# Sample-state steps moved from the levels of the triangular inverses to the steps of the chunk chain (RWKV-7 stage of a hybrid decoder trunk)

## Chip, cores, metric

One NeuronCore of one Trainium2 chip. The metric is the device time of one execution in microseconds (us). The time before is the median of three runs.

## What is computed

A two-layer trunk runs over 256 prompt tokens and 32 sample tokens (8 sequences of 4 tokens each, the "last tokens"). Layer 0 is a chunked gMLP unit and a SwiGLU. Layer 1 is RWKV-7 time mixing with 16 heads of 64, and then a top-2-of-8 expert SwiGLU. The change lies in the RWKV-7 recurrence:

```
def step(s, inp):
    r_t, w_t, k_t, v_t, kk_t, a_t = inp
    s_kk = jnp.einsum("bhij,bhj->bhi", s, kk_t)
    s = (s * w_t[:, :, None, :]
         - s_kk[..., None] * (kk_t * a_t)[:, :, None, :]
         + v_t[..., None] * k_t[:, :, None, :])
    y = jnp.einsum("bhij,bhj->bhi", s, r_t)
    return s, y
```

The prompt starts from a zero state. Each of the 8 samples starts from its own state (16 heads of 64x64). The outputs and the last states of both are outputs of the kernel.

## The kernel before

Every engine has its own instruction queue, written out in the order of the program. The recurrence isn't run token by token. The prompt is cut into four chunks of 64 tokens. Inside a chunk the recurrence becomes a triangular system, so the stage has three parts:

- **Scores and inverses.** For each half `i` (two chunks, all 16 heads), the step `score` makes the products of keys and queries, `xt0` and `x0` start an inverse, and five levels `t1/i/m`, `xl/i/m` (m = 1 to 5) build it up. A `t1` is a product that ScalarE copies out of PSUM in two halves (L1028). An `xl` is the product that follows, which VectorE copies by a mask into the inverse (L1545). On TensorE (PE) a `t1` is L2198 and an `xl` is L2213.
- **The chunk chain.** For chunk `c` = 0 to 3: `w1` (L2151, L2228, L2236), `u` (L2260 with L2247 and L2252), `s` (L2279) and `y` (L2288, L2291, L2294). Each one's result is copied out of PSUM (ScalarE L1033, L1038, L1043; VectorE L1551, L1556, L1569) before a later one reads it. From `c` = 1 on, `w1` has a second part that takes the same state to `y`, and `u` has products behind the ones that are copied.
- **The samples.** The steps whose names begin with `q_` do the same for the 32 sample tokens. `q_xt0`, `q_x0`, `q_t1` and `q_x2` are their small inverse. `q_s0/p` (p = 0 to 7, a pair of heads) turns the loaded states with four 128x128 transposes into bank 6 (L2343), from which ScalarE copies them (L1058). `q_qs/p` is the state times the sample's rows, 16 small matmuls a step with 2x4 = 8 moving columns each (L2351); after four of them ScalarE copies the sum (`Qs`, L1064), and GpSimd scales the state (L755). Then come `q_w1/g`, `q_u/g`, `q_y/g` (g = 0, 1 is a group of 8 heads; PE L2363 and L2367, L2375, L2384), and `q_st/p`, which makes the last state (PE L2401, L2409; ScalarE L1076) that four DMAs on SyncE's queue store (L592). GpSimd makes the key blocks of `q_st` (L739).

After the chain come the group norm (`gm`, `gv`: L2419, L2428) with `q_st/4` to `q_st/7` between its steps, then `gate`, `state` and the output projection `wo`.

What sets the order is one list, `steps` (L407 to L433). The main steps are appended one after the other by `then`, and after each one the next entry of the list `fill` is appended, which holds the sample steps. All engines walk the same list, each issuing its share of every step. The waits are worked out from the list, so a step that is moved keeps its own waits:

```
        def then(step):
            steps.append(step)
            steps.extend(fill.pop(0))
```

Bank 6 is one buffer, so a step `q_s0` waits until the copy of the one before has read it:

```
                    elif p == 4:
                        q_wait(pe, "q_qc", 0)
                    else:
                        q_wait(pe, "q_s0c", p - 1)
```

Of the kernel before, what the change touches and what calls it, by code (L numbers as in the profile page):

```python
# [54 lines left out]
def trunk_kernel(nc, a, out):  # L55

    with ExitStack() as ctx:
# [339 lines left out]
        def norm_dve(k, gain, dst):  # L397
            nc.vector.wait_ge(S["rinv_ready"], k)
            for c in range(DC):
# [7 lines left out]
        steps = [("score", 0, g_) for g_ in range(4)] + [("xt0", 0), ("q_score", 0), ("x0", 0), ("q_score", 1)]  # L407
        fill = [[("score", 1, 0)], [("score", 1, 1)], [("score", 1, 2)], [("score", 1, 3)], [("xt0", 1), ("q_xt0", 0)],
                [("q_x0", 0)], [("q_s0", 0)], [("q_t1", 0)], [("q_s0", 1)], [("q_x2", 0)],
                [("q_s0", 2)], [("q_x0", 1)], [("q_s0", 3)], [("q_t1", 1)], [("q_qs", 0), ("q_qs", 1)], [("q_x2", 1)],  # L410
                [("q_qs", 2), ("q_qs", 3)], [("q_w1", 0)], [], [("q_u", 0)], [("q_y", 0)],
                [("q_s0", 4)], [("q_s0", 5)], [("q_s0", 6)], [("q_s0", 7)],
                [("q_qs", 4), ("q_qs", 5)], [("q_qs", 6), ("q_qs", 7)], [("q_w1", 1)], [("q_st", 0)],
                [("q_u", 1)], [("q_st", 1)], [("q_y", 1)], [("q_st", 2)], [], [("q_st", 3)], [], []]

        def then(step):
            steps.append(step)
# [2257 lines left out]
```

## Time and profile before

| | |
|---|---|
| runs, us | 1540.66, 1546.23, 1542.77 (median 1542.77) |
| profiled execution: its own time, us | 1537.36 |
| its span, us | 1535.6 |
| TensorE busy | 1493.6 us (97%) |
| VectorE, ScalarE, GpSimd busy | 71%, 56%, 8% |
| mean granted TensorE clock | 0.992 |

The trace splits each of this stage's f32 matmuls in two records, so a step with 32 matmuls has 64 records. Ends of matmuls overlap the starts of the next by about 0.07 us in the timeline; the chain of waits cuts this overlap off.

### The profile page before, as it was taken

How to read it: one execution, taken by the hardware profiler on the slowest of the kernel's cores; microseconds unless marked ns; L12 is line 12 of the kernel's file. 1: busy time of each engine (PE TensorE's matmuls, PEld its weight loads, DVE VectorE, ACT ScalarE, POOL GpSimd, SP SyncE). 2: the span in 40 equal slices, each digit the busy share in tenths (PEclk: the TensorE clock that was granted, in tenths of full speed). 3: DMA queues.
4: the chain of work that ended last, by engine and by line, in shares of the span. 5: the costliest groups of instructions: out<-in, count | busy, mean ns of one | idle time of the engine just before them, and what ended most of it. 6: DMA issues, size and time to landing. Idle time of an engine off the chain costs nothing.

```text
span 1535.6 us, 26614 instructions
## 1 busy us (share of the span) xinstructions
PE 1493.6 (97%) x11533; PEld 1219.1 (79%) x11533; DVE 1090.4 (71%) x1053; ACT 857.2 (56%) x838; POOL 130.5 (8%) x170
## 2 busy tenths in 40 slices
PE   7999999999999979999999999999999999999997
PEld 7999999999889768976667777777777777777774
DVE  5687455554468664222498888888889889888897
ACT  5444444433264323232367777777777777777775
POOL 0065100000100030142000000000000000000010
PEclk9999999999999999999999999999999999999999
DMA  8643575535255020055599999999999999999992
GB/s 261 186 138 83 164 228 165 165 114 160 74 164 166 1 58 4 21 127 182 193 313 390 377 381 371 367 388 373 376 369 373 382 381 376 367 380 367 385 388 89
DMA packets 250269, 378.05 MB, mean 246 GB/s; under 512 B 28169, under 2 KB 142073, under 8 KB 249858
## 3 DMA queue, kind: packets, MB, share of 16 engines
q1 hardware_dynamic: 247874, 370.04, 69.5%
q0 software_dynamic: 2064, 6.18, 1.2%
q8 instruction: 93, 1.52, 0.4%
q14 instruction: 30, 0.25, 0.1%
q10 hardware_dynamic: 208, 0.07, 0.0%
HBM read 368.47 MB, written 7.78 MB: 245 GB/s over the span
## 4 chain that ended last, share of the span: by engine, by line
PE 94%; DVE 3%; issue 1%; ACT 1%; DMA 0%; ACTq 0%; DVEq 0%
PE bank L2552 46%; PE bank L1916 27%; PE bank L2039 3%; PE bank L2213 1%; PE bank L2198 1%; DVE wL L1609 1%; PE bank L2460 1%; PE bank L2485 1%; PE bank L2561 1%; PE bank L1969 1%; PE bank L2409 1%; PE bank L2533 1%; PE bank L2401 0%; PE bank L2351 0%; PE bank L2260 0%
## 5 line engine op out<-in xcount | busy, mean ns | idle before, releaser
L1609 DVE TENSOR_TENSOR wL<-ering,wH 128x2048 fp32r<-128x2048 f32 x264 | 603.6, 2289 | 87.7 <-ACT wH L1102 86.3
L1102 ACT ACTIVATE wH<-ering 128x2048 fp32r<-128x2048 f32 x264 | 506.0, 1917 | 152.4 <-PE bank L2552 151.5
L2552 PE MATMUL bank<-wH,xgH 128*96 128x512 f32 (+1 forms) x768 | 290.2, 378 | 3.1 <-DVE wL L1609 2.8
L2552 PE MATMUL bank<-wH,xgL 128*96 128x512 f32 (+1 forms) x768 | 287.3, 374 | 0.0
L2552 PE MATMUL bank<-wL,xgH 128*96 128x512 f32 (+1 forms) x768 | 286.9, 374 | 0.0
L2552 PEld LDWEIGHTS bank<-wH,xgH 128*96 128x96 f32 x768 | 124.4, 162 | 46.5 <-issue 3.1
L2552 PEld LDWEIGHTS bank<-wH,xgL 128*96 128x96 f32 x768 | 124.2, 162 | 43.9
L2552 PEld LDWEIGHTS bank<-wL,xgH 128*96 128x96 f32 x768 | 124.5, 162 | 41.4
L2552 PE MATMUL bank<-wH,hH 128*96 128x512 f32 x352 | 139.5, 396 | 0.5 <-DVE wL L1609 0.5
L2552 PE MATMUL bank<-wH,hL 128*96 128x512 f32 x352 | 138.3, 393 | 0.0
L2552 PE MATMUL bank<-wL,hH 128*96 128x512 f32 x352 | 137.9, 392 | 0.0
L906 ACT ACTIVATE fwH<-fring 128x2048 fp32r<-128x2048 f32 (+1 forms) x38 | 64.2, 1690 | 116.8 <-PE bank L1916 116.8
L1352 DVE TENSOR_TENSOR fwL<-fring,fwH 128x2048 fp32r<-128x2048 f32 (+1 forms) x38 | 76.4, 2011 | 42.7 <-ACT fwH L906 42.7
L1916 PE MATMUL bank<-fxH,fwH 128*128 128x288 f32 x352 | 104.4, 297 | 0.0
L1916 PE MATMUL bank<-fxH,fwL 128*128 128x288 f32 x352 | 103.8, 295 | 0.0
L1916 PE MATMUL bank<-fxL,fwH 128*128 128x288 f32 x352 | 103.5, 294 | 0.0
L1916 PE MATMUL bank<-inH,inW 128*128 128x288 f32 x256 | 77.3, 302 | 0.5 <-DVE inL L1298 0.5
L2552 PEld LDWEIGHTS bank<-wH,hL 128*96 128x96 f32 x352 | 56.7, 161 | 24.7
L2552 PEld LDWEIGHTS bank<-wH,hH 128*96 128x96 f32 x352 | 56.8, 161 | 24.6 <-DVE wL L1609 1.4
L1916 PE MATMUL bank<-inH,lowW 128*128 128x288 f32 x256 | 76.1, 297 | 0.0
L1916 PE MATMUL bank<-inL,inW 128*128 128x288 f32 x256 | 75.9, 296 | 0.0
L2552 PEld LDWEIGHTS bank<-wL,hH 128*96 128x96 f32 x352 | 56.9, 162 | 22.8
(431 smaller groups left out, 2557.3 us busy)
## 6 DMA issues: line engine op xcount, KB each, us to landing
ering<-m_w_gate SPq DMA_DIRECT2D x88, 1024.0 KB, 7.0
ering<-m_w_up SPq DMA_DIRECT2D x88, 1024.0 KB, 7.4
ering<-m_w_down SPq DMA_DIRECT2D x88, 1024.0 KB, 7.4
arena<-a_w_in SPq DMA_DIRECT2D x16, 1024.0 KB, 5.7
arena<-b_w_rkv SPq DMA_DIRECT2D x12, 1024.0 KB, 5.2
fring<-f_w_gate SPq DMA_DIRECT2D x11, 1024.0 KB, 5.4
fring<-f_w_up SPq DMA_DIRECT2D x11, 1024.0 KB, 5.3
fring<-f_w_down SPq DMA_DIRECT2D x16, 704.0 KB, 4.7
```

What stands on the lines that cost most here:

```text
L906: nc.scalar.activation(fw[n % FRING][0][:, 0:w], fring[:, (F_GU + n) % RING, 0:w], ACT.Copy) \
L1102: s_.activation(wH[:, hslot(g), :], ering[:, eslot(g), :], ACT.Copy).then_inc(S["e_hi"], 1)
L1352: v.tensor_tensor(fw[n % FRING][1][:, 0:w], fring[:, (F_GU + n) % RING, 0:w], fw[n % FRING][0][:, 0:w].bitcast(F32), ALU.subtract).then_in ...
L1609: v.tensor_tensor(wL[:, hslot(g), :], ering[:, eslot(g), :], wH[:, hslot(g), :].bitcast(F32), ALU.subtract).then_inc(S["e_lo"], 1)
L1916: mm = t.matmul(bank[:, 0:T], w2[l], x2[r][:, k, :], start=(start and m == 0), stop=(stop and m == 2))
L1969: mm = t.matmul(banks[c % 4][:, t0:t0 + n], vtok[0:n, i, P * c:P * c + P], w, start=False, stop=True, skip_group_check=True)
L2039: mm = t.matmul(bank, w(k), x[:, k, :], start=(k == 0), stop=(k == ks - 1))
L2198: mm = t.matmul(banks[3 * f][far, 64 * j:64 * j + 64], MS[ch, BL, i, 8 * f + j, :], X[ch, 8 * f + j, :], start=(j == 0), stop=True, skip_g ...
L2213: mm = t.matmul(banks[1 + 3 * f + x][ch if x else far, 64 * j:64 * j + 64], pair[x], pair[1 - x], start=(j == 0), stop=True, skip_group_ch ...
L2409: mm = t.matmul(bank[:, P * q:P * q + P], S0[p][:, 2 * q:2 * q + 2, :].rearrange("p b i -> p (b i)"), ident[:, :], start=False, stop=True, ...
L2460: mm = t.matmul(banks[4 + c][:, 0:T], wo[c // 2][:, k_, P * (c % 2):P * (c % 2) + P], yT[:, k_, :], start=(k_ == 0), stop=(k_ == DC - 1))
L2552: mm = t.matmul(dst, lhs[l], rhs[r], start=(start and m == 0), stop=(stop and m == 2), skip_group_check=True)
```

## The change

Only the list `fill` changes. `q_qs/0` to `q_qs/3`, `q_w1/0`, `q_u/0` and `q_y/0` no longer stand between the levels of the second inverse (`t1/1/m`, `xl/1/m`), but between the steps of the chain. What stood in the chain moves down by up to several steps to make room: `q_st/0` to `q_st/3` move down by two steps of the chain each, `q_st/3` from between `u/3` and `s/3` to behind `y/3`. `q_s0/4` and `q_s0/5` now follow each other directly. From `gm/0` on both lists are the same, and so is everything up to `xl/1/2`.

```diff
@@ -407,11 +407,10 @@
         steps = [("score", 0, g_) for g_ in range(4)] + [("xt0", 0), ("q_score", 0), ("x0", 0), ("q_score", 1)]
         fill = [[("score", 1, 0)], [("score", 1, 1)], [("score", 1, 2)], [("score", 1, 3)], [("xt0", 1), ("q_xt0", 0)],
                 [("q_x0", 0)], [("q_s0", 0)], [("q_t1", 0)], [("q_s0", 1)], [("q_x2", 0)],
-                [("q_s0", 2)], [("q_x0", 1)], [("q_s0", 3)], [("q_t1", 1)], [("q_qs", 0), ("q_qs", 1)], [("q_x2", 1)],
-                [("q_qs", 2), ("q_qs", 3)], [("q_w1", 0)], [], [("q_u", 0)], [("q_y", 0)],
-                [("q_s0", 4)], [("q_s0", 5)], [("q_s0", 6)], [("q_s0", 7)],
-                [("q_qs", 4), ("q_qs", 5)], [("q_qs", 6), ("q_qs", 7)], [("q_w1", 1)], [("q_st", 0)],
-                [("q_u", 1)], [("q_st", 1)], [("q_y", 1)], [("q_st", 2)], [], [("q_st", 3)], [], []]
+                [("q_s0", 2)], [("q_x0", 1)], [("q_s0", 3)], [("q_t1", 1)], [], [("q_x2", 1)], [], [], [], [], [],
+                [("q_qs", 0), ("q_qs", 1)], [("q_qs", 2), ("q_qs", 3)], [("q_w1", 0)], [("q_s0", 4), ("q_s0", 5)],
+                [("q_u", 0), ("q_s0", 6)], [("q_s0", 7)], [("q_y", 0), ("q_qs", 4), ("q_qs", 5)], [("q_qs", 6), ("q_qs", 7)],
+                [("q_w1", 1)], [("q_st", 0)], [("q_u", 1)], [("q_st", 1)], [("q_y", 1)], [("q_st", 2)], [], [("q_st", 3)]]
```

The list is one line shorter, so all later lines have a number that is one lower in the changed kernel (L2213 is L2212 there).

**First place:** TensorE at the second inverse, from `xl/1/2` to `w1/0`. Before (L2213 is `xl`, L2351 `q_qs`, L2198 `t1`, L2330 `q_x2`, L2363 and L2367 `q_w1`, L2375 `q_u`, L2384 `q_y`, L2151 `w1`):

```order
L2213 MATMUL bank<-arena 64x64 x64
L2351 MATMUL bank<-arena 64x2x4 x32
L2198 MATMUL bank<-arena 64x64 x32
L2330 MATMUL bank<-arena 32x32 x8
L2213 MATMUL bank<-arena 64x64 x64
L2351 MATMUL bank<-arena 64x2x4 x32
L2198 MATMUL bank<-arena 64x64 x32
L2363 MATMUL bank<-arena 32x64 x8
L2367 MATMUL bank<-ident,arena 32x128 x4
L2213 MATMUL bank<-arena 64x64 x64
L2198 MATMUL bank<-arena 64x64 x32
L2375 MATMUL bank<-arena 32x64 x8
```

The same stretch of the changed kernel, up to `u/0`:

```order
L2212 MATMUL bank<-arena 64x64 x64
L2197 MATMUL bank<-arena 64x64 x32
L2329 MATMUL bank<-arena 32x32 x8
L2212 MATMUL bank<-arena 64x64 x64
L2197 MATMUL bank<-arena 64x64 x32
L2212 MATMUL bank<-arena 64x64 x64
L2197 MATMUL bank<-arena 64x64 x32
L2212 MATMUL bank<-arena 64x64 x32
L2150 MATMUL bank<-arena 64x64 x32
L2350 MATMUL bank<-arena 64x2x4 x32
```

Only `q_x2/1` is left between the levels, `w1/0` follows the last level directly, and the first `q_qs` pair comes behind `w1/0`.

**Second place:** TensorE behind `y/0` (its last products are L2294, L2293 in the changed kernel), up to `w1/1`. Before:

```order
L2294 MATMUL bank<-arena 64x64 x8
L2343 MATMUL bank<-ident,arena 128x128 x4
L2228 MATMUL bank<-arena 64x64 x16
L2236 MATMUL bank<-arena 64x64 x16
L2351 MATMUL bank<-arena 64x2x4 x32
```

The changed kernel:

```order
L2293 MATMUL bank<-arena 64x64 x8
L2342 MATMUL bank<-ident,arena 128x128 x8
L2227 MATMUL bank<-arena 64x64 x16
L2235 MATMUL bank<-arena 64x64 x16
L2374 MATMUL bank<-arena 32x64 x8
```

One `q_s0` became two in a row (x8), and `q_u/0` (L2374) stands where `q_qs/4` and `q_qs/5` stood.

**Third place:** TensorE from the last products of `y/3` to the first of `gm`. Before:

```order
L2294 MATMUL bank<-arena 64x64 x8
L2419 MATMUL bank<-arena,halves 128x288 x2
L2401 MATMUL bank<-arena 64x4x64 x4
L2409 MATMUL bank<-ident,arena 128x128 x4
L2428 MATMUL bank<-arena,halves 128x288
```

The changed kernel:

```order
L2293 MATMUL bank<-arena 64x64 x8
L2400 MATMUL bank<-arena 64x4x64 x4
L2408 MATMUL bank<-ident,arena 128x128 x4
L2418 MATMUL bank<-arena,halves 128x288 x2
L2400 MATMUL bank<-arena 64x4x64 x4
```

`q_st/3` (L2400, L2408) now stands between `y/3` and `gm/0`.

## Rows read from the trace of the kernel before

**Rows 1.** Page, part 1, and the clock line of part 2 (40 slices):

```profile
PE 1493.6 (97%) x11533; PEld 1219.1 (79%) x11533; DVE 1090.4 (71%) x1053; ACT 857.2 (56%) x838; POOL 130.5 (8%) x170
PEclk9999999999999999999999999999999999999999
```

**Rows 2.** Windows: stretch, length, busy (count) per engine, PEclk, DMA share, GB/s

```profile
576.00:601.00 25.00, 24.61 (x869) 22.18 (x866) 10.36 (x16) 10.59 (x20) 0.00 (x0) 1.00 0.02 5
604.20:611.70 7.50, 7.50 (x223) 7.32 (x223) 1.17 (x2) 1.19 (x2) 1.58 (x2) 0.55 0.02 4
625.20:676.30 51.10, 49.68 (x1224) 45.55 (x1224) 10.57 (x17) 13.44 (x23) 11.75 (x8) 1.00 0.12 21
```

**Rows 3.** Waits of TensorE, 625 to 677 us: total us, times, longest

```profile
PE bank L2419 <- ACT arena L1043: 0.7, 1, 0.7
PE bank L2409 <- PE bank L2401: 0.6, 4, 0.2
PE bank L2151 <- DVE arena L1545: 0.4, 1, 0.4
```

**Rows 4.** Chain of waits, 590 to 680 us: start us, us, what

```profile
593.20 0.62 PE bank L2316 x16
...
601.07 1.27 issue
...
602.67 1.65 PE bank L2351 x58
...
611.68 1.77 PE bank L2351 x58
...
617.34 2.02 PE bank L2213 x128
619.37 1.99 PE bank L2198 x64
...
635.14 0.59 PE bank L2343 x4
...
637.80 1.69 PE bank L2351 x57
...
661.56 0.44 PE bank L2384 x16
...
678.71 1.13 PE bank L2409 x8
```

**Rows 5.** ScalarE's timeline at `y/0`, `q_s0/7`: start us, us, instruction [idle]

```profile
635.18 0.60 ACT L1043 ACTIVATE arena<-bank 128x512 f32<-128x512 f32 x1 [1.41 <-PE bank L2294]
635.77 0.60 ACT L1058 ACTIVATE arena<-bank 128x512 f32<-128x512 f32 x1
```

**Rows 6.** Chain of waits around `w1/0`: start us, us, what

```profile
624.42 0.74 DVE arena L1545
625.20 2.19 PE bank L2151 x63
627.41 0.60 ACT arena L1033
628.05 0.27 PE bank L2260
```

**Rows 7.** Timelines of VectorE and ScalarE at `xl/1/4` and `t1/1/5`

```profile
618.47 0.75 DVE L1545 COPY_PREDICATED arena<-arena,bank 128x512 f32<-128x512 int32 x1 [4.78 <-PE bank L2213]
619.40 1.95 DVE L1545 COPY_PREDICATED arena<-arena,bank 128x512 f32<-128x512 int32 x3 [0.19 <-PE bank L2213]
620.47 0.60 ACT L1028 ACTIVATE arena<-bank 128x512 f32<-128x512 f32 x1 [2.50 <-PE bank L2198]
```

**Rows 8.** SyncE's queue: sample stores from 680 us on, and its later waits (640 to 760 us)

```profile
680.50 15.90 SPq L592 DMA_DIRECT2D out_wkv_sample<-arena  x16
...
SPq L554 <- PE bank L2449: 13.2, 1, 13.2
...
SPq L594 <- ACT arena L1091: 4.1, 1, 4.1
```

## Prediction

> **What bounds the kernel now.** I read the page first. TensorE is busy 97% of the span and the others far less [rows 1], so a reordering can gain only where TensorE stands still or runs slowly. The clock line of the page is full in every slice, but a slice is 38 us, so a short fall doesn't show; the windows do. Second, the windows around the steps that move [rows 2]: before the moved steps, TensorE is busy 24.61 of 25.00 us, and in the chain, from `w1/0` at 625.20 to `gm/0` at 676.30, 49.68 of 51.10. Third, the waits in the chain [rows 3]: 0.7 us before `gm/0` (ScalarE's copy of `y/3`), 0.4 before `w1/0` (VectorE's last copy of the inverse), and four of 0.16 (0.6) inside `q_st`, between its own two halves. That is all that a filler could cover, and the last kind stays wherever `q_st` stands. So the chain isn't short of work to hide its copies, and the inverses aren't either.
>
> Fourth, the chain of waits [rows 4] and the windows show the one large loss near the change. After 1.27 us in which TensorE waited for nothing that the profile shows ("issue"), and the sparse `q_qs/0` and `q_qs/1`, the granted clock falls: its mean from 604.20 to 611.70 is 0.55 [rows 2], that is 1.2 GHz in nine tenths of the stretch. It runs `t1/1/3`, `q_x2/1` and `xl/1/3`.
>
> **The change, part by part.** All instructions stay; only their places move. TensorE's work is therefore the same and the sum is one of gaps and clock.
>
> 1. *The levels lose their fillers.* Four boundaries become bare: `xl/1/2` to `t1/1/3`, `xl/1/3` to `t1/1/4`, `t1/1/4` to `xl/1/4`, and `t1/1/5` to `xl/1/5`. One of this kind is bare already, `xl/1/4` to `t1/1/5`: 617.34 + 2.02 = 619.36, and `t1/1/5` starts at 619.37 [rows 4]. It needs VectorE's first copy, done at 618.47 + 0.75 = 619.22 [rows 7], so it holds by 0.15. For `t1` to `xl`, `t1/1/5` would end at 619.37 + 1.99 = 621.36; its first half has been copied at 620.47 + 0.60 = 621.07, and the second of VectorE's three copies, which the first half of `xl` needs too, ends at 619.40 + 2 x 0.65 = 620.70 [rows 7]. It holds by 0.3. I take 0. The other end is the 0.60 to 0.75 of one copy laid bare at each of the four, 3 us in all; the rows are at the zero end.
>
> 2. *`q_y/0` no longer lies before `w1/0`.* `w1/0` waits for the last masked copy, 624.42 + 0.74 = 625.16, and starts at 625.20 [rows 6], with or without `q_y/0`. So there its 0.44 (the size of `q_y/1` in [rows 4]) was hidden. Behind `s/1` it is laid on top: **+0.44**.
>
> 3. *Behind `w1/0`* ScalarE's copy ends at 628.01 and `u/0` starts at 628.05 [rows 6]. The `q_s0` between them ends at 625.20 + 2.19 + 0.59 = 627.98, so 0.07 is bare. With a `q_qs` pair (1.69, [rows 4]) in its place the copy of 0.60 is covered: **-0.07**.
>
> 4. *`q_s0/5` directly behind `q_s0/4`.* Both write bank 6. Now the same situation, `y/0` and one `q_s0` behind it, looks so: `q_s0` runs on TensorE 635.14 to 635.73 [rows 4]; ScalarE first copies `y/0` (635.18), then bank 6 from 635.77 to 636.37 [rows 5]. A second `q_s0` can't start before 636.42 (0.05 from a copy's end to the start that waits on it, by [rows 6]). TensorE's queue is in order, so `w1/1`, `q_u/0` and all behind it stand too: 636.42 - 635.73 = **+0.69**. Nothing of it is given back, as no later copy is waited for in the chain.
>
> 5. *`q_st/3` behind `y/3`.* Its second half alone takes 1.13 [rows 4], so it covers the 0.6 of the copy of `y/3`, for which `gm/0` waits. The 0.7 there [rows 3] goes: **-0.69**. Between `u/3` and `s/3` stands `q_st/2` instead, as long as `q_st/3`, so nothing is bared.
>
> 6. *The other queues.* ScalarE has the same copies; behind each chain step it does that step's copy first, as the list has it there. `q_w1/0` needs the copy of `Qs` after `q_qs/3`, with `s/0` and its own first half between; `q_w1/1` needs it after `q_qs/7`, with `w1/2` between. GpSimd's four scalings and four key blocks take 11.75 of the chain's 51.10 us [rows 2]; four more scalings come into it and a key block leaves, and what each makes is used by a `q_st` two or more chain steps later. On SyncE's queue the store of `q_st/3` (four DMAs, about 1.0 each by 15.90 / 16 in [rows 8]) now comes behind the three weight loads instead of before them. The sixteen stores behind it are issued back to back, so the last ones come up to 4 us later; the queue then idles 4.1 us for L594 [rows 8]. I cost it at nothing; this cover is almost used up, and the next thing behind is the one store of 256 KB (L594) and the last weight piece, which waits another 13.2 us [rows 8].
>
> Gaps together: 0.44 - 0.07 + 0.69 - 0.69 = **+0.37 us**.
>
> 7. *The clock.* From the end of `q_qs/1` at 602.67 + 1.65 = 604.32 to `q_qs/2` at 611.68 there is one `t1`, one `q_x2` and one `xl` [rows 4]. At full clock they take 1.99 (619.37), 0.62 (593.20, of the same shape as `q_x2`) and 2.02 (617.34), together 4.63. They took 611.68 - 604.32 = 7.36, so the fall cost 2.7 us. What TensorE did before it: 1.27 us of nothing, then 1.7 us of matmuls with 8 moving columns. The `q_qs` pair at 637.80, with no pause before it, wasn't followed by a fall: the chain's window is at 1.00 throughout [rows 2]. In the changed kernel the place of the pause is followed by `t1/1/3` at once, with 64 moving columns in each matmul, and the sparse pairs stand in the chain, where no pause like it was seen. I take the fall to go away: **-2.7**. The ends are 0 (it stays, or another takes its place) and -2.7.
>
> The Trainium skill (TensorE: Matmul & The Clock Gate, "HAM oscillation — how this bites in real kernels") puts such falls down to pauses of TensorE and tells one to remove these; sparse matmuls aren't in its rule. By it the fall belongs to the pause at 601.07, which the change leaves where it is, and the sum would be +0.37 alone.
>
> **The sum.** -2.73 + 0.37 = -2.36 us. The profiled execution took 1537.36, which gives 1535.0. The median of the runs is 5.4 above it, with runs from 1540.66 to 1546.23, so other stretches differ between executions by more than this change is worth. On the median: 1542.77 - 2.36 = **1540.4 us**. A measurement of this kernel can tell about 0.3%, 4.6 us, from no change; the forecast lies within that.
>
> **The rivals.**
>
> *The fall stays with the pause.* For it: clock falls elsewhere in this trace follow waits too, and the pause lies in instructions that don't move. Against it: TensorE was at work from 602.34 on, about 2 us or more before the fall. Only the gaps count: 1542.77 + 0.37 = 1543.1. The same number comes out if one fall in the chain takes the place of the old one. This is also how it would look if the reordering did nothing. Chance 0.33.
>
> *Slower: the sparse steps pull the clock down in the chain.* `q_qs/0` to `q_qs/3` stand on either side of `u/0`, and `q_qs/4` to `q_qs/7` on either side of `y/1`, the second group right behind the short `q_y/0`. In the kernel before, the first two pairs are 7.4 us apart; now only one chain step lies between the pairs of a group. If each group brings a fall of 2.7 and the old one stays as well, the time is 1542.77 + 0.37 + 2 x 2.7 = 1548.5. It decides as slower only from the second additional fall on, with the old one staying. For it: the old fall did follow such a pair. Against it: the two pairs that are in the chain already, one of them at 637.80, didn't bring one. With some chance of bared copies at the levels (part 1) I give it 0.08.
>
> *Much faster.* The fall goes, and the 1.27 us of issue with it, since the instructions behind it differ: -2.7 - 1.27 + 0.37 = -3.6, 1539.2. It takes scatter in addition to pass 4.6. Chance 0.09. The forecast itself has 0.5.
>
> **The numbers.** Forecast 1540.4, and the scatter of a median of such runs is about 2.8 to each side (half of 5.57). The range takes in the forecast less 2.8 and half of the rival's gain, 1536.5, and the first rival plus 2.8, 1546.0. Faster by over 0.3% needs a median under 1538.1: 0.15, the upper tail of the forecast's scatter and the last rival. Slower by over 0.3% needs over 1547.4: 0.10. Within: 0.75.
>
> **What would show it.** TensorE's line 2212 and 2197 at the levels back to back, with no gap over 0.1 us; a wait of 0.8 to 0.9 before L2150; a wait of 0.6 to 0.7 of L2342 on ScalarE between the two `q_s0` behind `y/0`; no wait of L2418 on ScalarE; the granted clock at 1.00 from 576 to 700. From the first instruction after the issue pause to `gm/0` the stage should be 2.4 us shorter. The prediction is wrong if the levels show waits on VectorE or ScalarE (part 1), if a fall appears behind a `q_qs` pair in the chain (part 7), or if the time differs by over 4.6 us from a place outside this stage.

## The result, and the profile after

The changed kernel takes 1551.57 us (median of 20 runs, 1544.52 to 1558.08), the kernel before 1541.97 (20 runs, 1537.79 to 1554.86). The ratio is 1.0061, with a 95% interval from 1.0047 to 1.0075: slower by 9.6 us. The forecast was 1540.4 in a range of 1536.5 to 1546.0, with the "slower" rival at 0.08.

The page of the changed kernel, first line, parts 1 and 2 (compare [rows 1]):

```profile
span 1552.8 us, 26614 instructions
...
PE 1507.3 (97%) x11533; PEld 1229.1 (79%) x11533; DVE 1090.5 (70%) x1053; ACT 857.3 (55%) x838; POOL 131.6 (8%) x170
...
PEclk9999999999999999899899999999999999999999
```

Every engine has the instructions it had. TensorE is busy longer by 13.7 us (its weight loads by 10.0, the other engines by at most 1.1), and two slices of the clock line are lower than before: the 17th (621 to 660 us, this stage) and the 20th (738 to 776, behind it, where the kernel before has a fall too, too short for its slice to show). A "fall" is a stretch in which the granted clock is at the lower level. Slices are 39 us wide, so the windows have to say where. Stretch, length, busy time (count) of PE, PEld, DVE, ACT, POOL, then PEclk, DMA share, GB/s:

```profile
607.40:624.10 16.70, 13.14 (x533) 12.40 (x533) 8.02 (x12) 3.58 (x6) 0.00 (x0) 1.00 0.11 35
624.08:690.40 66.32, 64.98 (x1408) 60.01 (x1409) 10.75 (x17) 14.41 (x25) 14.02 (x11) 0.85 0.09 17
633.90:641.90 8.00, 7.31 (x68) 6.01 (x65) 0.00 (x0) 1.78 (x3) 0.00 (x0) 0.52 0.01 2
641.90:654.60 12.70, 12.70 (x334) 11.95 (x333) 2.96 (x5) 3.56 (x6) 0.20 (x1) 0.90 0.01 3
654.60:664.80 10.20, 10.20 (x186) 10.20 (x184) 0.69 (x1) 1.57 (x3) 3.96 (x4) 0.51 0.01 4
```

The first row is the levels of the second inverse, from the pause in `xl/1/2` to `w1/0`; the second is the chain, `w1/0` to `gm/0`. In the chain the mean granted clock was 1.00 before [rows 2] and is 0.85 now. It stands near 1.2 GHz in two stretches: from `q_w1/0` to `w1/1`, and from `y/1` behind `q_qs/4` and `q_qs/5` to `w1/2`. The old fall at `t1/1/3` is gone: the levels run at 1.00.

The waits of TensorE in both stretches, 606 to 691 us (compare [rows 3] and the 1.27 us of issue in [rows 4]): total, times, longest.

```profile
PE bank L2212 <- issue: 3.7, 3, 1.7
PE bank L2150 <- DVE arena L1544: 0.8, 1, 0.8
PE bank L2197 <- issue: 0.7, 1, 0.7
PE bank L2342 <- ACT arena L1057: 0.7, 1, 0.7
PE bank L2408 <- PE bank L2400: 0.7, 4, 0.2
```

The gaps are the ones forecast: 0.82 before `w1/0`, 0.69 between the two `q_s0`, none before `gm/0`. But the pauses for which the profile names no cause ("issue") have grown from 1.27 to 4.4 us. The chain of waits shows where they lie and how slow steps became:

```profile
605.69 1.74 issue
...
610.13 0.84 PE bank L2212 x44
610.98 0.40 issue
611.38 1.50 PE bank L2212 x81
612.88 1.32 PE bank L2197 x44
614.20 0.74 issue
614.94 0.74 PE bank L2197 x18
615.74 1.63 PE bank L2212 x104
617.37 1.57 issue
...
634.08 1.63 PE bank L2366 x8
...
637.62 1.70 PE bank L2293 x16
...
666.40 0.99 PE bank L2366 x8
```

The pauses fall inside a `t1` or an `xl`, not at the boundaries that were laid bare. They have a distance of their own: from the end of one to the end of the next TensorE ran 127, 128 and 127 matmul records, in 3.6 to 4.0 us each time. Windows from end to end of the four pauses:

```profile
607.42:611.38 3.96, 3.55 (x127) 3.31 (x128) 1.17 (x2) 1.19 (x2) 0.00 (x0) 1.00 0.01 4
611.38:614.94 3.56, 2.82 (x128) 2.68 (x127) 2.69 (x4) 0.60 (x1) 0.00 (x0) 1.00 0.02 5
614.94:618.93 3.99, 2.42 (x127) 2.29 (x127) 0.74 (x1) 0.60 (x1) 0.00 (x0) 1.00 0.02 4
```

The second part of `q_w1/0` (L2366) takes 1.63 us where that of `q_w1/1` takes 0.99: the price of the lower clock, step by step.

All experiments change this one stage, and what lies ahead of it varies between executions. So their profiles are compared over one stretch, from `x0/1` (its products of 512 columns) to the first product of `gm/0`. It holds the same steps in every one of them, and is 87.9 us before (588.38 to 676.30) and 97.6 in the changed kernel (592.76 to 690.40): 9.7 us, by chance the same as the difference of the medians. The two profiled executions differ by 17.2 us (1537.36 and 1554.54), for the one of the kernel before lies 4.6 us under its median and the one of the changed kernel 3.0 above. Of the rest, 4.4 us lie ahead of the stretch and 3.1 behind it. From `gm/0` to the end the kernel before takes 859.3 us and the changed one 862.4, with a longer fall behind this stage (granted clock 0.66 from 757 to 782 us; 0.86 from 747 to 772 before).

### The profile page after: what moved, and what is told of

Its sections match the earlier page's. It is cut to its first block, busy times and chain, and to the rows that moved or that the text cites. A ratio compares the mean times of both kernels' runs of the same rounds, so it can differ in the third digit from the quotient of the medians.

```text
span 1552.8 us, 26614 instructions
## 1 busy us (share of the span) xinstructions
PE 1507.3 (97%) x11533; PEld 1229.1 (79%) x11533; DVE 1090.5 (70%) x1053; ACT 857.3 (55%) x838; POOL 131.6 (8%) x170
## 4 chain that ended last, share of the span: by engine, by line
PE 93%; DVE 3%; issue 2%; ACT 1%; DMA 0%; ACTq 0%; POOL 0%; DVEq 0%; POOLq 0%
PE bank L2551 45%; PE bank L1915 27%; PE bank L2038 3%; PE bank L2212 1%; PE bank L2197 1%; DVE wL L1608 1%; PE bank L2459 1%; PE bank L2484 1%; PE bank L2560 1%; PE bank L2532 1%; PE bank L1968 1%; PE bank L2408 1%; PE bank L2350 1%; PE bank L2027 0%; PE bank L2086 0%
```

## The experiments

Where a median is given, the kernel before ran beside it, and the ratio is to that. Medians of different experiments, and the 1551.57 of the changed kernel, come from different sets, and each ratio is known to 0.0014 to 0.0027 (2 to 4 us) to either side.

**r1, r2: both kernels once more, unchanged.**

> The kernel before, unchanged, profiled a second time, to see what in its stage is the same each time. Theory C (clock): the fall of the granted clock behind q_qs/0 and q_qs/1 belongs to the place and is seen again within a few us of t1/1/3. Theory P (pauses belong to the instruction stream): the 1.27 us of issue inside xl/1/2 is seen again at the same place, to within 0.5 us. Rival (both are chance): neither is at its old place. From the first score step to the first gate step the stage took 148.5 us; it is expected at 145.5 to 149 again.

> The changed kernel, unchanged, profiled a second time. Its stage from the first score step to the first gate step took 160.2 us, 2.8 of it by a fall at 555 us that lies before the change. Theory C: both falls in the chain (from q_w1/0 to w1/1, and from q_qs/4 to w1/2) come again, 4 to 4.5 us each. Theory P: the pauses of 0.4, 0.7 and 1.6 us in the bare levels come again, 2.7 in all. Rival: chance, and the stage takes about 149.

The kernel before, second profile (windows of the levels and the chain, then its waits, 601 to 678 us):

```profile
603.00:626.00 23.00, 20.24 (x715) 19.11 (x715) 9.15 (x15) 5.14 (x9) 4.17 (x4) 1.00 0.11 32
626.07:677.10 51.03, 49.59 (x1225) 45.47 (x1225) 10.56 (x17) 13.44 (x23) 11.74 (x8) 1.00 0.12 21
```

```profile
PE bank L2213 <- issue: 2.2, 2, 1.2
...
PE bank L2198 <- issue: 0.5, 1, 0.5
```

The fall is not there, and yet the stretch from `x0/1` to `gm/0` is 87.2 us, 0.7 less than with it, not 2.7. In its place stand pauses: 2.7 us instead of 1.27. Against the expectation of theory C the fall doesn't come each time at its place; whether it comes is a matter of the execution (in e9 and e10, below, whose levels are the same, it starts within a microsecond of the end of `q_qs/1`, as in the kernel before; in e7 it is missing). The first pause is at its old place again (0.99 instead of 1.27), and the two others end 255 and 128 matmul records further on:

```profile
603.76:611.40 7.64, 6.46 (x255) 6.13 (x255) 2.27 (x4) 1.19 (x2) 2.08 (x2) 1.00 0.02 4
611.40:615.41 4.01, 3.52 (x128) 3.38 (x128) 1.95 (x3) 0.98 (x2) 2.09 (x2) 1.00 0.01 4
```

So it is the same spacing as in the changed kernel, with one pause left out, although other steps stand between. By these counts the places of the pauses go with the number of instructions, and what differs between the profiles is how long each pause is. From the first `score` step to the first `gate` the stage took 149.4 us, where 145.5 to 149 was expected.

The changed kernel, second profile:

```profile
602.75:619.65 16.90, 13.36 (x531) 12.57 (x532) 8.39 (x13) 3.58 (x6) 0.00 (x0) 1.00 0.13 40
619.65:683.52 63.87, 62.53 (x1408) 57.69 (x1409) 10.74 (x17) 14.40 (x25) 14.02 (x11) 0.89 0.09 15
646.50:661.50 15.00, 15.00 (x244) 14.11 (x243) 0.69 (x1) 2.16 (x4) 3.65 (x4) 0.54 0.01 3
```

The stretch is 94.7 us. There is a single long fall, over the second group of `q_qs`, instead of two; the pauses in the levels are 3.6 us. So both losses come again, in other sizes. Behind `gm/0` this execution takes 863.0 us, against 859.1 in r1.

**e1, e3: `q_qs` cut, in the changed kernel and in the old order.** Only the first sequence's product is made; the rest of the sum is left out.

```diff
-                    for b in range(NB):
+                    for b in range(1):
                         for ch in BOTH:
```

> The changed kernel with q_qs cut from 16 matmuls to 2 (only the first sequence's product is made, the rest of the sum is left out), in all eight steps, so that the sparse stretches shrink from 1.7 to about 0.2 us a pair. The work left out is 4 x 1.5 = 6 us. Theory C (the sparse pairs bring the clock down in the chain): both falls go as well, 8.5 us more, so the time is 14 to 15 below the changed kernel, about 1537. Rival (the falls have another cause, the waits in the chain): only 6 below, about 1545.5, and the falls are still there. The pauses in the bare levels stay 2.7 us under both.

> The kernel before with q_qs cut from 16 matmuls to 2 as in the cut of the changed kernel (the same part of the sum is left out). The work left out is 6 us. The changed kernel lost 17 us by this cut. Theory C (the change's loss is the clock that the sparse pairs bring down in the chain): in the old order the pairs bring down little, so the cut gives 6 to 8, about 1535, and the two cut kernels lie within 3 us of each other, where the whole ones are 9.6 apart. Rival (the cut helps any order alike, and the loss comes from the order itself): the cut gives 17 here too, about 1525.5, and the 9.6 between the orders stays.

Changed order, cut: 1534.45 us (ratio 0.9950, 0.9933 to 0.9967). Old order, cut: 1535.95 us (0.9952, 0.9935 to 0.9969). The same cut gives 17.1 us in the changed order and 7.3 in the old one (6 of it the work itself), and the 9.6 between the orders is gone. (The 6 us is an estimate, 4 x 1.5.) The chain of each, windows of e1 and of e3:

```profile
625.59:677.67 52.08, 50.06 (x1184) 45.73 (x1185) 10.74 (x17) 14.30 (x25) 14.02 (x11) 1.00 0.10 19
```

```profile
624.86:673.67 48.81, 46.61 (x1112) 42.40 (x1112) 10.58 (x17) 13.45 (x23) 11.75 (x8) 1.00 0.14 23
```

Both are at 1.00. By the medians the order by itself costs nothing that the runs can tell from none (1.5 us less, each ratio known to 2.6 us); the large loss comes only together with the sparse matmuls of `q_qs`. The two profiles show that the order still costs something: from `x0/1` to `gm/0` e1 takes 83.9 us and e3 80.9. Of these 3.0 us, 1.9 are pauses (4.7 against 2.8 us in the stretch) and 1.1 copies laid bare, the largest of them behind `w1/0`, 0.7, where the cut steps are too short to cover ScalarE's copy. Both profiled executions are the slowest of their twelve (1542.64 and 1539.25), so they show this stage and not the typical time.

**e2: `q_qs/0` to `q_qs/3` back between the levels, the rest as changed.**

```diff
-... [("q_t1", 1)], [], [("q_x2", 1)], [], [], [], [], [],
-[("q_qs", 0), ("q_qs", 1)], [("q_qs", 2), ("q_qs", 3)], [("q_w1", 0)], ...
+... [("q_t1", 1)], [("q_qs", 0), ("q_qs", 1)], [("q_x2", 1)], [("q_qs", 2), ("q_qs", 3)], [], [], [], [],
+[], [], [("q_w1", 0)], ...
```

> The changed kernel with only q_qs/0 to q_qs/3 put back between the levels, as before; q_w1/0, q_u/0, q_y/0 and all others stay in the chain. Theory C: the first fall in the chain (4.3 us) goes, the old fall behind t1/1/3 (2.7) comes back, the second (4.5) stays; w1/0 and u/0 lose their cover, about +0.9. Theory P (TensorE's instructions arrive at a limited rate, about 35 pairs of load and matmul per us, and the levels with q_qs but without q_w1 and q_u need more): the pauses in the levels are as large as in the changed kernel or larger, 2.5 to 4 us. Together 1549 to 1551. Rival (the bare boundaries themselves, and not instructions per us, make the pauses): with two boundaries filled the pauses halve.

1549.65 us (1.0051, 1.0035 to 1.0068). Window of its chain, and TensorE's waits from 600 to 686 us:

```profile
626.31:684.76 58.45, 56.31 (x1281) 51.83 (x1281) 10.75 (x17) 14.03 (x24) 9.84 (x7) 0.94 0.09 17
```

```profile
PE bank L2212 <- issue: 3.8, 3, 1.5
PE bank L2150 <- DVE arena L1544: 0.8, 1, 0.8
PE bank L2259 <- ACT arena L1032: 0.7, 1, 0.7
```

As theory C had it, the first fall in the chain goes, a short one comes in the levels (behind `q_qs/2` and `q_qs/3`), and one stays over the second group. As theory P had it, the pauses are as large as in the changed kernel though two boundaries are filled again; a pair of `q_qs` brings 64 matmul records of its own. The 0.7 before `u/0` (L2259) is ScalarE's copy of `w1/0`, which nothing covers here.

**e4: `q_qs` spread singly over the chain.** These lines replace the last three of the changed list.

```diff
+                [("q_qs", 0)], [("q_qs", 1)], [("q_qs", 2)], [("q_qs", 3)],
+                [("q_w1", 0)], [("q_s0", 4)], [("q_u", 0), ("q_s0", 5)], [("q_s0", 6)],
+                [("q_y", 0), ("q_s0", 7)], [("q_qs", 4)], [("q_qs", 5)], [("q_qs", 6)],
+                [("q_qs", 7)], [("q_w1", 1)], [("q_st", 0)], [("q_u", 1), ("q_st", 1), ("q_y", 1), ("q_st", 2), ("q_st", 3)]]
```

> The changed kernel with the eight q_qs spread singly over the chain, one per chain step, never two in a row; the steps between and behind them move down with them. Theory C in its narrow form (it takes sparse stretches of 1.7 us close to each other): the falls go or one short one is left, and the stretch from x0/1 to gm/0 takes 88 to 92 us instead of 94.7 and 97.6; time 1543 to 1547. Rival (any q_qs between the chain's steps brings the clock down, as their share is the same): falls as long as in the changed kernel, 1550 or more.

1548.42 us (1.0044, 1.0021 to 1.0067), 1.4 more than theory C's narrow form allowed. It is 3 us less than the changed kernel's median, which the intervals don't separate. The stretch from `x0/1` to `gm/0` is 91.3 us, 3.3 and 6.3 less than in the changed kernel's two profiles; 0.7 of it is the wait between the two `q_s0`, which no longer stand together. The chain:

```profile
622.71:683.53 60.82, 60.08 (x1408) 55.40 (x1409) 10.85 (x17) 14.41 (x25) 14.02 (x11) 0.94 0.15 42
```

Falls are shorter in this profile, but single `q_qs` still bring some; that spreading helps the time is not shown.

**e5: dense matmuls behind each `q_qs`.**

```diff
                     mm.then_inc(S["q_pe"], 1)
+                    q_wait(pe, "q_yc" if p >= 4 else "q_x2c", 0 if p >= 4 else 1)
+                    for q in range(4):
+                        t.matmul(banks[7][:, P * q:P * q + P], ident[:, :], ones[:, :],
+                                 start=(q == 0), stop=True, skip_group_check=True)
                 elif k == "q_w1":
```

> The changed kernel with four dense matmuls of 128 rows, 128 columns (0.59 us, into bank 7, whose contents are not used) behind each of the eight q_qs, so that TensorE has 4.7 us more work and a wait of about 0.5 for q_y/0's copy before the first of the second group. Theory C: the falls go, 6 to 8 us, so the time is 1 to 3 us below the changed kernel in spite of more work, about 1549, with the clock at 1.00 through the chain. Rival (the falls don't come from the sparse matmuls): 5 us above it, 1556.5.

1552.45 us (1.0071, 1.0047 to 1.0095). The added work was mis-sized: I had taken the 0.59 us of four transposes, but a true f32 product has two records here where a transpose has one, and four take 1.08 us (625.33 to 626.41):

```profile
625.33 1.16 PE L2356 MATMUL bank<-ones,ident 128*128 128x128 f32 x8
626.41 0.27 PE L2259 MATMUL bank<-arena 64*64 64x64 f32 x1
```

```profile
620.48:687.79 67.31, 65.97 (x1472) 60.60 (x1473) 10.75 (x17) 14.40 (x25) 14.02 (x11) 1.00 0.09 16
```

So 8 x 1.08 = 8.6 us were added, and the median rose by 0.9, which can't be told from none. The clock is 1.00 through the whole chain. Without the added work this chain would be 67.31 - 8.6 = 58.7 us; it was 66.3 and 63.9 in the two profiles of the changed kernel. The falls cost it 7.6 and 5.2 us. This is the lower end: a `q_qs` with the dense matmuls behind it takes about 1.0 us here, half of a pair 0.85. The chain of e10 (below, 50.4 us, no fall) with the moved steps and gaps added (two `q_qs` pairs 3.4, `q_w1/0` 2.0, `q_u/0` 1.0, `q_y/0` 0.44, gaps 0.62) gives 57.8, and falls of 8.5 and 6.1.

**e6: few, dense matmuls at the four bare boundaries of the levels.**

```diff
-... [("q_t1", 1)], [], [("q_x2", 1)], [], [], [], [], [],
+... [("q_t1", 1)], [("pad", 0)], [("q_x2", 1)], [("pad", 0)], [("pad", 0)], [], [("pad", 0)], [],
...
+                elif k == "pad":
+                    q_wait(pe, "q_s0c", 3)
+                    for q in range(4):
+                        t.matmul(banks[6][:, P * q:P * q + P], ident[:, :], ones[:, :],
+                                 start=(q == 0), stop=True, skip_group_check=True)
```

> The changed kernel with four dense matmuls (0.59 us each time, into bank 6, contents not used) at the four boundaries of the second inverse that the change laid bare: 2.4 us more work in only 16 more pairs of load and matmul. Theory P (TensorE's instructions arrive at about 35 pairs per us, and the bare levels of 528 pairs in 13 us ask for more): the added work takes the place of the pauses, and from the pause in xl/1/2 to w1/0 the stretch stays at 16.7 to 17.4 us (16.7 and 16.9 in the changed kernel's two profiles). Rival (the pauses have nothing to do with how dense the instructions are): it grows by 2.4 to 19.1 or more. The time stays at 1551.6 within a microsecond, or rises by 2.4.

1554.43 us (1.0081, 1.0055 to 1.0108; 6 runs). The fillers are 4 x 1.08 = 4.3 us, not 2.4. The levels:

```profile
603.36:621.55 18.19, 17.37 (x563) 16.37 (x563) 8.41 (x13) 3.58 (x6) 0.00 (x0) 1.00 0.13 41
```

```profile
PE bank L2212 <- issue: 1.0, 1, 1.0
PE bank L2150 <- DVE arena L1544: 0.8, 1, 0.8
```

4.3 us of added work made the stretch 1.3 to 1.5 us longer (16.7 and 16.9 in the changed kernel), and the pauses behind the first, 2.7 and 2.6 us there, are gone; the 1.0 that is left is the first one, ahead of the fillers. The pauses weren't at the boundaries but filling the boundaries removed them. Theory P holds; its number was off by the size of the filler. The saving doesn't show in the median, which lies 2.9 above the changed kernel's.

**e7, e8: the second group alone.** e7 is the kernel before with only the tail of the list as changed; e8 the changed kernel with `q_qs/6` and `q_qs/7` one step further down.

```diff
 e7, against the kernel before
-                [("q_qs", 4), ("q_qs", 5)], [("q_qs", 6), ("q_qs", 7)], [("q_w1", 1)], [("q_st", 0)],
-                [("q_u", 1)], [("q_st", 1)], [("q_y", 1)], [("q_st", 2)], [], [("q_st", 3)], [], []]
+                [], [], [("q_qs", 4), ("q_qs", 5)], [("q_qs", 6), ("q_qs", 7)], [("q_w1", 1)], [("q_st", 0)],
+                [("q_u", 1)], [("q_st", 1)], [("q_y", 1)], [("q_st", 2)], [], [("q_st", 3)]]
 e8, against the changed kernel
-... [("q_y", 0), ("q_qs", 4), ("q_qs", 5)], [("q_qs", 6), ("q_qs", 7)],
-                [("q_w1", 1)], [("q_st", 0)], [("q_u", 1)], [("q_st", 1)], [("q_y", 1)], [("q_st", 2)], [], [("q_st", 3)]]
+... [("q_y", 0), ("q_qs", 4), ("q_qs", 5)], [],
+                [("q_qs", 6), ("q_qs", 7)], [("q_w1", 1)], [("q_st", 0)], [("q_u", 1), ("q_st", 1)], [("q_y", 1)], [("q_st", 2)], [], [("q_st", 3)]]
```

> The kernel before with only the second half of the list changed as in the changed kernel: q_qs/4 and q_qs/5 behind s/1 and q_qs/6 and q_qs/7 behind y/1 (2.0 us between the pairs, where it was 4.3), and q_w1/1, q_st/0 to q_st/3 as in the changed kernel. The levels and the first q_qs pairs are as before. Theory C, with the distance of the pairs as what matters: a fall comes behind the second group in most executions, 2 to 4.5 us, less the 0.7 before gm/0 that is now covered, so the time is 1544 to 1546. Rival (only the first group in the chain or the bare levels matter): 0.7 below before, 1541.5, and no fall.

> The changed kernel with q_qs/6 and q_qs/7 moved one step further down, behind w1/2, so that 4 us of dense steps (y/1, w1/2) lie between the second group's pairs; q_w1/1 and q_st/0 move one step too. Theory C, by distance: the fall behind the second group goes or is rarer, so 2 to 4 us less than the changed kernel, 1547.5 to 1549.5. Rival (the distance of the pairs doesn't matter, only that they are in the chain): 1551.5.

e7: 1546.85 us (1.0034, 1.0016 to 1.0052), 4.5 above the kernel before that ran beside it. e8: 1546.96 us (1.0028, 1.0010 to 1.0047), 4.6 below the changed kernel. Their chains:

```profile
627.46:685.48 58.02, 57.28 (x1224) 52.77 (x1225) 10.66 (x17) 12.86 (x22) 9.86 (x7) 0.85 0.09 16
```

```profile
621.46:687.57 66.11, 64.78 (x1409) 59.40 (x1410) 10.75 (x17) 14.41 (x25) 14.02 (x11) 0.85 0.09 17
```

Both medians came out as the distance theory had them or nearly so (e7 0.9 above its range, e8 0.5 below), and e7 shows that moving the second group alone costs about half of the loss. But the profile of e8 has falls as long as the changed kernel's (and a time of its own of 1549.14), and the trace speaks against distance within the group. In e8 the second fall starts as `q_qs/5` ends, at 654, and is over when `q_qs/6` starts, at 660.7:

```profile
654.00:660.60 6.60, 6.60 (x112) 6.60 (x111) 0.69 (x1) 1.19 (x2) 1.39 (x2) 0.50 0.01 4
```

In r2 too it has begun before `q_qs/6` starts at 648.8, with TensorE never idle:

```profile
644.60:646.80 2.20, 2.20 (x89) 2.20 (x85) 0.89 (x2) 0.00 (x0) 0.82 (x1) 1.00 0.00 0
646.80:648.80 2.00, 2.00 (x42) 2.00 (x39) 0.00 (x0) 0.00 (x0) 1.27 (x2) 0.67 0.04 8
```

The same holds in the changed kernel's first profile, in e2, e6 and e7. A pair that hasn't run yet can't have set off the fall, so the distance to it can at most lengthen one. What made e8's median lower is not shown.

**e9, e10: the kernel before with only `q_st/3` behind `y/3`, twice.**

```diff
-                [("q_u", 1)], [("q_st", 1)], [("q_y", 1)], [("q_st", 2)], [], [("q_st", 3)], [], []]
+                [("q_u", 1)], [("q_st", 1)], [("q_y", 1)], [("q_st", 2)], [], [], [], [("q_st", 3)]]
```

> The kernel before with only q_st/3 moved behind y/3, the one part of the change whose wait the trace shows. All theories: the 0.69 us before gm/0 goes and nothing else changes, so x0/1 to gm/0 takes 86.5 to 87.2 us (87.9 and 87.2 before) and the time is 1541.5 to 1542.5, which the runs can't tell from before. If instead the time rises by over 3 us, moving q_st/3 past the weight loads on SyncE's queue has a cost that was put at nothing.

> The kernel before with q_st/3 behind y/3, a second time, since the first left a ratio of 0.9987 with an interval up to 1.0003, and its profile showed a fall of 6.8 us in the chain that no profile of the kernel before has. Theory C, with falls as a matter of chance in each execution: the profile lies between 86.5 and 94 us from x0/1 to gm/0, the median between 1538.5 and 1542. If the gain of 3.5 us in the first set is real and not chance, the median is again under 1540; by the wait alone it is 0.7 below before.

1538.84 us (0.9987, 0.9972 to 1.0003), then 1541.00 (0.9998, 0.9978 to 1.0018). The wait before `gm/0` is gone in both profiles. The larger gain of the first set didn't come again; what is left agrees with the 0.7 of the wait and can't be told from none. The profile of e9 has what no profile of the kernel before had, a fall inside the chain, and takes 92.6 us from `x0/1` to `gm/0`, where 86.5 to 87.2 was expected:

```profile
624.90:681.34 56.44, 55.56 (x1224) 50.45 (x1225) 10.58 (x17) 12.84 (x22) 9.85 (x7) 0.88 0.11 19
646.00:660.50 14.50, 14.34 (x160) 12.20 (x159) 1.39 (x2) 2.37 (x4) 2.38 (x2) 0.53 0.09 15
```

Its execution took 1542.52 us, where eight of the twelve runs lie below 1539.1; e10's profile has no fall in the chain, took 1537.82 and has 86.6 us from `x0/1` to `gm/0`. So in the old order too the clock can fall in the chain. It did so in one of four profiles (before, r1, e9, e10), and in all seven with the second group moved, `q_qs` whole and nothing dense behind it (after, r2, e2, e4, e6, e7, e8).

## Why the prediction was wrong

*Parts 1 to 6, the gaps.* The boundaries of parts 2 and 4 to 5 came to within 0.05 us: 0.82 before `w1/0`, 0.69 between the two `q_s0`, no wait before `gm/0`. SyncE's queue idled 3.8 us before L593 instead of 4.1, so nothing was lost there. In part 1 no wait on VectorE or ScalarE appeared between the levels. But part 1 asked only who waits for whom. It took the bare levels to run at the pace of one step after another, and they didn't: the pauses grew to 4.4 and 3.6 us, from 1.3 and 2.7. The row was in front of me: 1.27 us of issue inside an `xl` [rows 4], and I let it stand as something that the change leaves alone. The levels from that pause to `w1/0` (602.34 to 625.20, 22.86 us before) should have come to 22.86 - 2.7 - 6.4 = 13.8 us (6.4 is the moved `q_qs`, `q_w1/0` and `q_u/0`) and took 16.7, of which 2.7 are the pauses behind the first.

*Part 7, the clock,* is the step that failed: -2.7 for a fall that goes, and nothing for falls that come. It took a fall to need two things, the pause and the sparse matmuls behind it, and so held the sparse pairs in the chain, without a pause, to be harmless. The falls in the chain came without one: in the changed kernel's first profile TensorE was busy 10.10 of the 10.10 us before the first of them, at 1.00:

```profile
624.10:634.20 10.10, 10.10 (x322) 9.94 (x323) 2.07 (x3) 1.56 (x3) 4.17 (x4) 1.00 0.06 19
```

That the old fall would go was so in both profiles, but -2.7 was never to be had: in r1 the kernel before ran without the fall and was 0.7 us quicker over the stretch, since at full clock the levels meet their pauses. The price was a little high too: the same steps (`t1/1/3`, `q_x2/1`, `xl/1/3`) took 6.24 - 1.18 = 5.1 us in r1 without their pause, not 4.63. And the clean window of the chain was one execution, which I read as if it were the rule. e5 and the pair e1 and e3 show that falls of 5 to 8 us in the chain come with the sparse matmuls and go when those are cut or have dense ones behind them.

*The rival that came true* is the slower one. It named the place and the mechanism, and was given 0.08 and a price of 2 x 2.7 with the old fall staying. The falls cost 7.6 and 5.2 us, and the old one did go. With the pauses as a second term it comes to the sum below. For its chance I leaned on the two pairs in the chain that hadn't brought a fall, though the change doubles their number there and puts them between other steps; e7 shows that moving the second group alone is worth 4.5 us.

*The Trainium skill's rule* that pauses of TensorE bring its clock down (TensorE: Matmul & The Clock Gate, "HAM oscillation — how this bites in real kernels") gave +0.37. That section works it out on waits for DMA between bursts of matmuls; putting it to a pause of 1.27 us was the prediction's own step. Measured was +9.6, with the chain's falls in stretches where TensorE waits for at most 0.7 us at a time. Pauses alone don't account for them.

*The sum as it should have been,* from `x0/1` to `gm/0`, means of two profiles each: gaps +0.4; pauses from 2.0 to 4.0, +2.0; old fall, about -1 (in one of the two profiles, 87.9 - 87.2 + 1.4 of pauses that it stood in for = 2.1 us); falls in the chain, about +6.4 by e5 and +7.3 by e10. Together +7.8 or +8.7. Measured over the stretch, (97.6 + 94.7) / 2 - (87.9 + 87.2) / 2 = +8.6; over the runs, +9.6. That these two lie close is in part luck. The same four profiles differ by another 3.5 us behind `gm/0`, where the changed kernel's fall of the clock lasts longer (862.4 and 863.0 us to the end, against 859.3 and 859.1), while both profiles of the kernel before lie over 4 us under its medians. The prediction put nothing there. The order alone doesn't decide it: e3, in the old order, takes 863.8 and e8 859.8.

What stays open: how often a fall comes in each order (a few profiles and the spread of the runs don't count them), which steps around a sparse pair make it bring a fall, whether the longer fall behind this stage comes from the change, and what TensorE waits for in its "issue" pauses.

## What to carry to other kernels

A filler has a density of its own. Before moving one, ask not only what it hides, but how many instructions per microsecond it brings to the place it goes to and takes from the place it leaves, and how sparse its matmuls are: here steps of 8 moving columns brought the clock down for longer once more of them stood between the chain's steps. A clean window around such a step in one profile doesn't make it harmless. And profile the kernel before a second time before costing a fall of the clock or a pause that has no releaser: it may be the execution's, and something else may take its place when it goes.

## What the runs showed of the hardware

TensorE's pauses named "issue" come where instructions are dense, and then at fixed distances: 127 or 128 pairs of load and matmul record (once 255) from one to the next in the changed kernel's first profile and in r1, although the steps between differ. From 576 to 601 us the kernel before ran 869 pairs in 25 us, 35 per us [rows 2], with one pause of 0.3. An `xl` alone has 128 pairs in 2.02 us, 63 per us, and the bare levels averaged 533 in 16.70 us, pauses included, 32 per us, with the ends of the pauses 3.6 to 4.0 us apart. 32 more pairs that take long (e6, 563 in 18.19 us) removed all but the first pause. The Trainium skill (Runtime: NRT & Kernel Launch, "Instruction fetch mechanics") says that fetching is hidden since issue is slower than the fill. If these pauses are fetches, which no run here shows, that doesn't hold for runs of small matmuls.

The clock can be low with TensorE busy throughout, behind and among matmuls that move few columns: over 654.60 to 664.80 us of the changed kernel it was busy 10.20 of 10.20 us, and the granted clock was 0.51. Before the fall that starts at about 634 us it had been busy for 10.10 of 10.10 us at 1.00. In the kernel before the clock fell where a sparse pair came behind a pause, in some executions (before, e9, e10) and not in others (r1, e7). Dense 128x128 products of 1.08 us behind each `q_qs` kept it at 1.00, and but for 0.9 us (within the noise) they paid for themselves.
